# Distances modulo 256 bytes between the weights and the rounded activations in SBUF

## The reference, cut to what matters

```python
xn = rms_norm(h, norm_mix_g[layer])
mix = even_mixer(xn, even_w_in[j], even_w_out[j], ...)   # xn @ w_in, attention, y @ w_out
h = h + mix
h = h + conv_gated_ffn(rms_norm(h, norm_ffn_g[layer]), ffn_w_up[layer], ...)  # x @ w_up, conv, silu(g) * u @ w_down
```

## The kernel before, in words

| tensor | byte modulo 256 | less the weights' |
|---|---|---|
| whi, wlo | 128 | 0 |
| xhi, xlo | 192, 64 | +64, -64 |
| zhi, zlo | 0, 128 | 128, 0 |
| hhi, hlo | 0, 0 | 128, 128 |
| mhi, mlo | 0, 0 | 128, 128 |
| o_hi, o_lo | 64, 64 | -64, -64 |
| hhi2, hlo2 | 128, 128 | 0, 0 |
| phi, plo | 128, 128 | 0, 0 |

## Time and profile before

### The profile page before, as it was taken

The page is one execution under the profiler, slowest core; times in us unless marked ns, Lnnn a source line. Parts: engine busy times, 40 slices in busy tenths (PEclk is TensorE's granted clock), DMA queues, the critical chain, the costliest instruction groups (busy, mean ns, idle before and its releaser), DMA issues.

```text
span 1296.2 us, 21549 instructions
## 1 busy us (share of the span) xinstructions
PE 1257.8 (97%) x8792; PEld 1156.8 (89%) x8792; DVE 840.6 (65%) x1454; ACT 702.3 (54%) x1161; POOL 238.4 (18%) x181
## 2 busy tenths in 40 slices
PE   8999999999999999999999999999988999999997
PEld 7787899998878799998899999999888989999885
DVE  6785588874664468886467777787854456555455
ACT  5555466653446556564356666666657435444334
POOL 2000000000000010000046665665425400000001
PEclk9999999999999999999979999999999999999999
DMA  8542355555443255555433322323212446555542
GB/s 311 220 144 102 113 195 195 177 181 180 164 161 130 70 205 203 189 195 196 134 130 131 131 89 108 130 99 111 86 66 96 182 163 231 174 189 196 183 145 78
DMA packets 31442, 200.29 MB, mean 155 GB/s; under 512 B 4272, under 2 KB 6464, under 8 KB 8560
## 3 DMA queue, kind: packets, MB, share of 16 engines
q1 hardware_dynamic: 29360, 189.79, 41.2%
q0 software_dynamic: 1840, 8.60, 1.7%
q10 hardware_dynamic: 144, 0.52, 0.1%
HBM read 197.85 MB, written 1.05 MB: 153 GB/s over the span
## 4 chain that ended last, share of the span: by engine, by line
PE 71%; issue 20%; DVE 4%; ACT 2%; DMA 1%; POOL 1%; SPq 0%; POOLq 0%; DVEq 0%; ACTq 0%
PE ps L1037 20%; PE ps L1035 20%; PE ps L1036 20%; PE ps L1399 1%; PE ps L1415 1%; DVE conv L2549 1%; PE ps L1051 1%; PE ps L1355 1%; DVE halves L2259 1%; DMA bias<-in_rel 1%; PE ps L1421 1%; PE ps L1360 0%; DMA x<-in_x 0%; DVE wlo L2173 0%; PE ps L1435 0%
## 5 line engine op out<-in xcount | busy, mean ns | idle before, releaser
L1035 PE MATMUL ps<-halves,whi 128*128 128x256 f32 x1472 | 420.1, 285 | 0.0
L1037 PE MATMUL ps<-halves,wlo 128*128 128x256 f32 x1472 | 416.4, 283 | 0.0
L1036 PE MATMUL ps<-halves,whi 128*128 128x256 f32 x1472 | 412.6, 280 | 0.0
L2173 DVE TENSOR_TENSOR wlo<-raw,whi 128x2048 fp32r<-128x2048 f32 (+2 forms) x144 | 324.9, 2258 | 131.8 <-ACT whi L1680 128.1
L1680 ACT ACTIVATE whi<-raw 128x2048 fp32r<-128x2048 f32 (+2 forms) x144 | 271.0, 1884 | 109.2 <-PE ps L1037 104.6
L1036 PEld LDWEIGHTS ps<-halves,whi 128*128 128x128 f32 x1472 | 279.9, 190 | 0.1
L1035 PEld LDWEIGHTS ps<-halves,whi 128*128 128x128 f32 x1472 | 278.8, 189 | 0.1
L1037 PEld LDWEIGHTS ps<-halves,wlo 128*128 128x128 f32 x1472 | 278.2, 189 | 0.0
L993 POOL TENSOR_TENSOR wlo<-raw,whi 128x1024 fp32r<-128x1024 f32 x72 | 173.7, 2419 | 62.3 <-ACT whi L1689 62.0
L921 POOL TENSOR_TENSOR rstd<-sumsq,half_power 128x1 f32<-128x1 f32 x16 | 12.4, 772 | 860.3 <-ACT xn L1707 673.7
L1035 PE MATMUL ps<-whi,halves 128*128 128x512 f32 (+4 forms) x432 | 151.4, 350 | 3.5 <-DVE halves L2259 3.4
(11 more groups left out here) (304 smaller groups left out, 1810.9 us busy)
## 6 DMA issues: line engine op xcount, KB each, us to landing
raw<-in_stream SPq DMA_DIRECT2D x176, 1024.0 KB, 4.8
gain<-in_gains POOLq DMA_DIRECT2D x7, 512.0 KB, 5.9
bias<-in_rel POOLq DMA_DIRECT2D x1, 1536.0 KB, 7.7
raw<-in_stream SPq DMA_DIRECT2D x2, 648.0 KB, 8.1
cst<-in_consts POOLq DMA_DIRECT2D x1, 1280.5 KB, 6.2
raw<-in_stream SPq DMA_DIRECT2D x2, 528.0 KB, 4.1
x<-in_x SPq DMA_DIRECT2D x2, 512.0 KB, 5.0
out<-xn SPq DMA_DIRECT2D x2, 512.0 KB, 2.6
```

The costliest lines, as they stand in the source:

```text
L1035: nc.tensor.matmul(out, a_hi, b_hi, start=start, stop=False)
L1036: nc.tensor.matmul(out, a_hi, b_lo, start=False, stop=False)
L1037: return nc.tensor.matmul(out, a_lo, b_hi, start=False, stop=stop)
L2173: dve.tensor_tensor(used(wlo, n), used(raw, n), used(whi, n).bitcast(F32), ALU.subtract)\
```

## The change

Three paddings and one offset grow by 32 elements, 128 bytes, each. No instruction is added, removed or moved, and no value changes.

```diff
-        halves = sb("halves", [P, 2, KT * TOK + 32], F32R)
+        halves = sb("halves", [P, 2, KT * TOK + 64], F32R)
         xhi, xlo = [halves[:, m, 0:KT * TOK].rearrange("p (k c) -> p k c", k=KT) for m in range(2)]
-        zhi, zlo = [halves[:, m, 16:16 + KT * TOK].rearrange("p (k c) -> p k c", k=KT) for m in range(2)]
+        zhi, zlo = [halves[:, m, 48:48 + KT * TOK].rearrange("p (k c) -> p k c", k=KT) for m in range(2)]
...
-            sb("space0", [P, 24], F32, area)
+            sb("space0", [P, 56], F32, area)
             hhi = sb("hhi", [P, FT, TOK], F32R, area)
...
-            sb("space2", [P, 24], F32, area)
+            sb("space2", [P, 56], F32, area)
             mhi = sb("mhi", [P, KT, TOK], F32R, area)
```

## The result

Ten runs of each kernel: 1295.55 us before, 1284.45 us after (1280.37 to 1290.82), a ratio of 0.9914 with a 95% interval of 0.9891 to 0.9937. The change gains 11 us, 0.9%; the forecast was 26.5. The profiled execution of the changed kernel took 1280.61 us (span 1278.8) against 1298.01 (span 1296.2), so 17.4 us less. The mean granted clock was 0.988 in the profile of before and 0.991 in that of after.

What follows compares the result with a forecast made beforehand. It took the kernel to be as long as PE's stream of matmuls, so pitch counts. The terms summed to 26.5 us off the profiled 1298.0, giving 1271.5, less 3.5 to the median: 1268.0 us, range 1262 to 1290.

Steps and rivals of the forecast that it cites:

- (c): down0 and down1: 528 matmuls at 512 columns, each 5.2 ns cheaper, 2.7 us.
- (d): Projections, mix_out and gate on zhi/zlo at 512 columns: 672 matmuls, each 6.3 ns cheaper, 4.2 us.
- (e): Output projections on mhi/mlo: 192 matmuls x 6.3 ns, 1.2 us, half taken because of waits, 0.6 us.
- (f): 96 matmuls of 324 and 264 columns on zhi/zlo: 4 ns each, 0.4 us.
- (a): The three up stages, 256 columns: 2880 matmuls, each 4.5 ns cheaper at a pitch of 113.3 ns, 13.0 us.
- (b): The rounds, 1536 matmuls: 4.4 us before 888, then 1.2 us, half of at most 2.5, where PE partly waits.
- (g): xhi/xlo as stationary under 256 columns (480 matmuls), pl_proj and delta_out: 0, at worst 2.2 us either way.
- B: Rival, chance 0.20: the 256-column streams gain nothing, only (c) to (f) remain, say 1288 us.
- C: Rival, chance 0.08: up stages and rounds get slower at +64; 1302.8 us at a 122 ns pitch, 1318 at 125.9.
- D: Rival, chance 0.06: positions in SBUF are no cause at all, time stays at 1294.5 us.

Runs made afterwards that it cites:

- g2_same: The changed kernel itself, unaltered, timed again beside the variant with p's transposes behind up2's last slot, with a third profile: 1282.3 us, ratio 0.9885.
- e4_halves_only: Only the change to halves and z, with paddings space0 and space2 back at 24 as in the kernel before: 1281.78 us in one execution.
- e8_again: The changed kernel itself, unaltered, a second execution profiled for its rhythms: 1284.43 us.
- e2_spins_plus: The changed kernel (x at +64) with 1, 2, 3 and 4 small identity matmuls before slots 6, 10, 14 and 18 of each up stage: 1301.45 us.
- e1_minus64: The changed kernel with xhi and xlo both at -64 against the weights instead of +64, other distances kept: 1280.99 us, ratio 0.9887.
- e3_spins_minus: The kernel with x at -64, plus 1, 2, 3 and 4 small identity matmuls before slots 6, 10, 14 and 18 of each up stage: 1291.91 us.

## Why the prediction was wrong

- *What bounds the kernel, and that pitches decide*: right. The spans differ by the pitches' sum, stage by stage, and delta_out and down2 kept theirs in the profile of after. delta_out was no safe control, as g2_same's profile shows.
- *(c) down, (d) z at 512 columns, (e), (f)*: nearly right. 1.5 and 1.4 us for 1.35 each; mix_out and the gate as forecast. In the projections the pitches in the blocks between attention's small products lie between 224 and 236 ns, mean 229, where before they had a mean of 233; the 6.3 ns a matmul were taken from mix_out, where nothing stands between. 1.6 us of the forecast went there.
- *(a) up stages*: right in up0 and up1 of the profile, 4.1 us each for 4.3, and wrong in up2.
- *The step that failed*: "neither sign costs by itself where the moving halves are alike ... I take 113.3". Halves alike and 64 bytes off do not give a pitch; they allow two, 113.3 and 118, and x at +64 with -64, as before the change, only the slow one. Distance decides what is possible; which of the two follows is decided at a restart, by something that the runs leave open. Term (a) lost 3.2 us to this and (b) most of its 5.6: with a restart in every half slot, only 3 in 10 of the rounds' matmuls are quick.
- *(b)*: 1536 matmuls times 4.5 ns would be 6.9 us, of which 1.3 were expected to turn into waits. The x matmuls gained 2.7 us in all, and the delta rule's small products took 1.4 more. That the 1.4 is the expected wait isn't shown: 16 more of the small ones started at the lower clock, and in g2_same's profile of the same kernel they take 136.8 us, as before the change.
- *(g)* held where it can be seen by itself: the z slots of the rounds take 22.6 us in both profiles.
- *From the profile to the median*: the forecast took 3.5 us off for the profile of before and let the changed kernel's median follow. That profile had a clock of 0.988; the one of after had 0.991 and lies 3.8 us below its median. So the profiles differ by 17.4 us and the medians by 11.1, and of the 15.4 us missing from the forecast, 9.1 are those of the table of stages, and 6.3 are where the two profiles lie among the runs.
- *Rivals*: B is what a part of each execution looks like, for another reason than it gave. C (122 ns) did not occur at +64, but at 0 and +96 there are 120 ns: an arrangement worse than before was near. D falls with down0 and with e4_halves_only. The Trainium skill, "SBUF — State Buffer", section "SBUF: two separate sides", has PE never wait for anyone; where 113.3 to 120.1 ns were measured for one shape by its operands' places alone, the measurement decides.
- *What the trace of before could have told.* delta_out was read as one number, 179 in 20 us. Its first starts are slower than the rest: 1021.37, 1021.49, 1021.60, 1021.73, then 0.11 apart from 1021.84 on. And of two z slots with equal distances the forecast used one; one that comes 53 us later begins at 118 ns and turns to 113 at its end:

```profile
761.09 0.28 PE L1036 MATMUL ps<-wlo,halves 128*128 128x256 f32 x1
...
761.80 0.28 PE L1036 MATMUL ps<-wlo,halves 128*128 128x256 f32 x1
...
762.14 0.28 PE L1036 MATMUL ps<-wlo,halves 128*128 128x256 f32 x1
```

Six pitches in 0.71 us, then three in 0.34, between neighbours of one loop. So the distance alone does not give the pitch even there: the first pitches behind an interruption are longer, which matters in the rounds, where most groups have 12 matmuls. It is not yet the two lasting rhythms. These first pitches give way within a dozen matmuls with nothing between, and delta_out, the one long stretch of before that moves 256 columns with halves alike, is quick past them. The lasting slow rhythm of halves alike showed only in the runs made after the prediction.

## What to carry to other kernels

Where PE is never idle, take the pitch of each shape from its starts, and compare stages that differ only in where operands lie: 5 ns a matmul, 4% at 256 columns and 2% at 512, were hidden there. Before one such pitch is carried to another stage, look at all stretches with the same operands and at what stands ahead of them; if they show two values, or if there is only one such stretch, forecast a mixture. Put the granted clock beside each time before a difference of some us is given to anything else. Of the distances tried here the best were: high and low halves at the same place modulo 256 bytes, level with the weights where 512 columns of them stream (against 128 bytes off), and 64 bytes off where 256 activations do.

## What the runs showed of the hardware

- 128x512 `F32R` matmuls, each with its own weight load: 227 ns at distance 0, 232 to 233 at 128 (both halves) and at 128 and 0 (high, low), 231.4 at 0 and 128. All these, and those below, at a granted clock of 1.00.
- 128x256, x moving, in the up stages: 120.0 at 0, 116.6 at +32, 113.3 or 118 at +64 and -64, 120.1 at +96, 118.7 at 128; 118 for +64 with -64 in either order. All but the values at 64 bytes are of one execution each.
- The two rhythms at 64 bytes last for over 900 matmuls and are exchanged only at interruptions of a few 100 ns: at -64 by 2, 3 and 4 small products but not by 1, in all three up stages of one execution; at +64 by one small product in up0 (quick to slow), not by the eleven other insertions, which came on a slow stream; at +64 by p's four transposes in both directions (quick to slow in after, e8_again and e4_halves_only, slow to quick in g2_same), though in e2_spins_plus they left up2 slow; at -64 they exchanged nothing (slow in e1_minus64, quick in e3_spins_minus).
- What sets the rhythm that a stage has from its second `turn_early` on is open, and so is the mechanism; it differs between executions of one program: up1 and delta_out are quick in the changed kernel's first profile and slow in g2_same's. That two reads of SBUF by TensorE meet in the same part of memory would fit the dependence on distance modulo 256 bytes, but no run here shows where they meet.
